# A two-layer attention, convolution and expert network on one core: the first attention scores are issued before the last two query tiles are rotated, and two normalisations are worked in halves of 256 tokens

## The reference

```python
def layer_norm(x, g, b):
    mu = xf.mean(-1, keepdims=True)
    var = jnp.square(xf - mu).mean(-1, keepdims=True)
    return (xf - mu) * lax.rsqrt(var + LN_EPS) * g + b
# each layer i
h = x * (1 + sc1) + sh1
mix = attention_mixer(...) if is_attn else short_conv_mixer(h, ...)
x = layer_norm(DEEPNORM_ALPHA * x + g1 * mix, ln_g[i, 0], ln_b[i, 0])
h = x * (1 + sc2) + sh2
ff = swiglu(h, w1, w3, w2) if is_dense else moe_swiglu(h, ...)
x = layer_norm(DEEPNORM_ALPHA * x + g2 * ff, ln_g[i, 1], ln_b[i, 1])
# in attention: q and k are rotated (apply_rope) before the scores q.k
```

## Time and profile before

| | |
|---|---|
| median of 3 runs | 2373.21 us (2371.28 to 2373.3) |
| time of the profiled execution | 2371.07 us |
| its span, first to last instruction | 2369.4 us |
| TensorE (PE) busy | 2256.5 us, 95% |
| PE weight loads | 1840.5 us, 78% |
| DVE / ACT / GpSimd busy | 62% / 46% / 14% |
| mean granted TensorE clock | 0.97 |

### The profile page before, as it was taken

One profiled execution on the slowest core, in us unless ns is written; L12 is line 12 of the kernel. 1 busy time (PEld: TensorE's weight loads), 2 busy tenths in 40 slices (PEclk: granted clock), 3 DMA queues, 4 the chain that ended last, 5 costly groups with the idle time before them and its releaser, 6 DMA issues.

```text
span 2369.4 us, 29554 instructions
## 1 busy us (share of the span) xinstructions
PE 2256.5 (95%) x11202; PEld 1840.5 (78%) x11203; DVE 1462.8 (62%) x1296; ACT 1096.2 (46%) x1084; POOL 324.9 (14%) x205
## 2 busy tenths in 40 slices
PE   6989999999998999798999999999999999999993
PEld 4866678888877888687888888888788788888782
DVE  3456655634566444897444454459999994544984
ACT  4135524222224222576343443347777774434763
POOL 0000026788852000100000000000000000000001
PEclk8999999999998999799999999999999999999997
DMA  7420083545442222798545554549999996454964
GB/s 306 190 107 1 1 339 125 195 167 187 178 146 92 100 89 89 288 379 308 213 177 195 187 209 179 198 183 398 360 394 366 394 371 230 179 193 177 359 261 143
DMA packets 76177, 512.71 MB, mean 216 GB/s; under 512 B 8241, under 2 KB 8369, under 8 KB 19025
## 3 DMA queue, kind: packets, MB, share of 16 engines
q1 hardware_dynamic: 61344, 442.46, 49.0%
q0 software_dynamic: 14768, 69.35, 8.0%
HBM read 482.41 MB, written 29.36 MB: 216 GB/s over the span
## 4 chain that ended last, share of the span: by engine, by line
PE 92%; DVE 4%; issue 1%; ACT 1%; DMA 1%; SPq 0%; DVEq 0%; ACTq 0%
PE ps L1672 27%; PE ps L1674 26%; PE ps L1673 26%; PE ps L562 2%; PE ps L517 2%; PE ps L573 2%; PE ps L2029 1%; DMA raw<-w_mod 1%; PE ps L1723 1%; PE ps L1774 1%; PE ps L521 1%; PE ps L1966 0%; DVE lo L1094 0%; PE ps L1822 0%; DVE zs L1267 0%
## 5 line engine op out<-in xcount | busy, mean ns | idle before, releaser
L1672 PE MATMUL ps<-ah,hi 128*128 128x512 f32 x688 | 270.4, 393 | 8.2 <-DVE al L1246 6.5
L1673 PE MATMUL ps<-al,hi 128*128 128x512 f32 x688 | 269.2, 391 | 0.0
L1674 PE MATMUL ps<-ah,lo 128*128 128x512 f32 x688 | 269.0, 391 | 0.0
L1538 DVE TENSOR_TENSOR he<-se,ps 128x512 f32<-128x512 f32 x112 | 77.0, 688 | 292.1 <-ACT se L993 291.8
L1295 DVE TENSOR_TENSOR lo<-raw,hi 128x2048 fp32r<-128x2048 f32 x112 | 255.9, 2284 | 0.0
L1672 PE MATMUL ps<-hia,xth 128*128 128x512 f32 x616 | 246.9, 401 | 6.9 <-issue 5.6
L1295 DVE TENSOR_TENSOR loa<-raw,hia 128x2048 fp32r<-128x2048 f32 x112 | 251.1, 2283 | 1.1 <-ACT hia L873 1.1
L1295 DVE TENSOR_TENSOR lob<-raw,hib 128x2048 fp32r<-128x2048 f32 x112 | 251.7, 2283 | 0.0
L993 ACT ACTIVATE se<-ps 128x512 f32<-128x512 f32 x112 | 67.0, 598 | 391.0 <-PE ps L1674 391.0
L1672 PE MATMUL ps<-hib,xth 128*128 128x512 f32 x616 | 245.4, 398 | 0.0
L1672 PE MATMUL ps<-hi,hh 128*128 128x512 f32 x616 | 240.5, 390 | 2.2 <-DVE hl L1542 1.5
(11 more groups left out here) (273 smaller groups left out, 3904.3 us busy)
## 6 DMA issues: line engine op xcount, KB each, us to landing
raw<-w_moe SPq DMA_DIRECT2D x336, 1024.0 KB, 5.4
raw<-w_pre SPq DMA_DIRECT2D x59, 1024.0 KB, 5.4
raw<-w_mod POOLq DMA_DIRECT2D x28, 1024.0 KB, 5.1
raw<-w_mod SPq DMA_DIRECT2D x20, 1024.0 KB, 7.5
dispatched_x<-zt POOLq DMA_DIRECT2D x22, 512.0 KB, 9.5
xg<-dispatched_x POOLq DMA_DIRECT2D x8, 1024.0 KB, 6.9
expert_y<-ys POOLq DMA_DIRECT2D x8, 1024.0 KB, 5.0
expert_y<-zt POOLq DMA_DIRECT2D x6, 512.0 KB, 24.6
```

What stands on the lines that cost most here:

```text
L1538: dve.tensor_tensor(HE[:], SE[:], up_view(q, 1), ALU.mult).then_inc(he_ready, 1)
L1672: pe.matmul(outp, wh, ah, start=first, stop=False, skip_group_check=True)
L1673: pe.matmul(outp, wh, al, start=False, stop=False, skip_group_check=True)
L1674: return pe.matmul(outp, wl, ah, start=False, stop=last, skip_group_check=True)
```

## The change

It touches the three places.

1. *Attention entry.* The last query unit writes banks 2 and 5 and TensorE goes on to the scores without waiting for its two rotations (`rope_done` 8 instead of 10; 10 is waited for at step 6, which first reads tile 6). The two `rope_tile` calls are issued by DVE in steps 1 and 2 of attention (`late`), the `split` of the first `o` unit in step 5. The last `mod_pair` and two `mod_cols` go behind the scores of step 1.
2. *Two normalisations by halves.* The last unit of `o` and of `dn2` is computed in four quarters (tokens 0 to 255 for both tiles, then tokens 256 to 511), of 24 matmuls of 256 tokens each. Residual, sums, squares, moments and the whole chain to `AL` run per half. `units_by_row_tile` runs once per half too, with matmuls of 256 tokens. `ZS` and `QS` now take in all 8 tiles, so 4 moment matmuls per half replace 24 in all.
3. *Moved splits.* The `split` of the next stage's second unit (slot 1) is issued before the tiles of the third unit of `o` and `dn2`; that of its first unit (slot 0) between the half tiles; ACT's `full_split` of the third unit between row tiles 5 and 6 of the second half. `scale_x` leaves the normalisation: in `up0` ACT does 8 half tiles after gated tile 1 and 8 after gated tile 2, in `conv` 16 before the third unit.

```diff
-        def attention_dve(dve, tn):
+        def attention_dve(dve, tn, late):
+                if s in late:
+                    late[s]()
-        def attention_pe(pe):
+        def attention_pe(pe, second_done):
-            pe.wait_ge(rope_done, 10)
+            pe.wait_ge(rope_done, 8)
+                if s == 6:
+                    pe.wait_ge(rope_done, 10)
+                if s == 1:
+                    second_done()
...
+                    late = {1: first_late, 2: lambda: rope_tile(2, Q[:, KD - 2, :], pair_free[1]),
+                            5: lambda: split(svs[0], svs[0])}
...
+            def last_unit(stage, gate):
+
+                half_tile(stage, 0, KD - 2, gate)
+                split(0, 0)
+                half_tile(stage, 0, KD - 1, gate)
+                half_tile(stage, 1, KD - 2, gate)
+                half_moments(stage, 0)
+                half_tile(stage, 1, KD - 1, gate)
+                dve.sem_inc(pair_free[1], 1)
+                half_norm(stage, 0)
+                half_norm(stage, 1)
...
+                        if name in ("o", "dn2") and j + 2 == ns:
+                            split(1, 1)
                         if lastpart and j + 1 == ns:
...
+            def half_stats(stage, h):
+                n = 2 * (stage - 1) + h + 1
+                if h == 0:
+                    pe.wait_ge(mod_free, t.n("mod"))
+                pe.wait_ge(stats_in, n)
+                for col, src in ((0, ZS), (1, QS)):
+                    for b in range(2):
+                        at = 4 * h + 2 * col + b
+                        ins = pe.matmul(PS[:, 7, at:at + 1], src[:, (2 * h + b) * BLK:(2 * h + b + 1) * BLK], mean_w[:, 0:1],
+                                        start=True, stop=True, skip_group_check=True)
                 ins.then_inc(stats_full, 1)
...
+            def unit_by_half(h, stage, ah, al):
+                for part in range(2):
+                    at = half_cols(part)
+                    for c in range(2):
+                        if part:
+                            pe.wait_ge(z_ready, n + KD - 2 + c + 1)
+                        for k in range(KD):
+                            ins = three(PS[:, 2 + c, at], hi[:, k, c * P:(c + 1) * P], lo[:, k, c * P:(c + 1) * P],
+                                        ah[:, k, at], al[:, k, at], k == 0, k == KD - 1)
+                        ins.then_inc(unit_done[h] if (part, c) == (1, 1) else part_done, 1)
+                        if (part, c) == (1, 0):
+                            half_stats(stage, 0)
+                half_rows(stage, 0)
...
+            def units_by_half(slots, part, stage):
+
+                half_stats(stage, 1)
+                units_by_row_tile(slots, part, (2 * stage - 1) * KD, half_cols(0), False, stage)
+                units_by_row_tile(slots, part, 2 * stage * KD, half_cols(1))
...
+                            if j in (1, 2):
+                                for k in range(KD):
+                                    scale_x(1, j - 1, k)
```

More of the change, by code:

```diff
@@ new lines, in normalised @@
+            def normalised(stage):
+                n = 2 * (stage - 1)
+                for k in (KD - 2, KD - 1):
+                    square(k, half_cols(0))
+                square(KD - 2, half_cols(1))
+                half_deviation(n + 1, 0)
+                square(KD - 1, half_cols(1))
+                for k in range(KD):
+                    if k == KD - 2:
+                        half_deviation(n + 2, 1)
+                    modulated(stage, 0, k)
+                for k in range(KD):
+                    modulated(stage, 1, k)
+                    if k == 5:
+                        full_split(2, 2)
@@ L918, in _ @@
                     full_split(0, 0)
+                    for h in range(2):
+                        for k in range(KD):
+                            scale_x(2, h, k)
                     done(2)
@@ L968, in _ @@
                         mod_part(1)
-                    if name in NORMS:
+                    if name in ("o", "dn2") and j + 1 == ns:
+                        normalised(NORMS[name])
+                    elif name in NORMS:
                         square(2 * j)
                         square(2 * j + 1)
[L972 to L978, removed]
+                if name == "co":
+                    deviation(5)
+            act.wait_ge(shift_ready, 5)
             for i in range(4):
@@ L1228, in norm @@
-                dve.wait_ge(rstd_rows, stage)
+                    dve.tensor_tensor(XZ[:, k, cols_], XZ[:, k, cols_], PS[:, bank, HALF:T], ALU.add).then_inc(xn_ready, 1)
+                dve.wait_ge(norm_rows, i + 1)
                 scaled(0)
-                dve.wait_ge(shift_rows, stage)
                 shifted(0)
@@ L1233, in norm @@
                 for k in range(1, KD):
+                    if h == 0 and k == KD - 2:
+                        half_moments(stage, 1)
                     if k + 1 < KD:
@@ L1313, in _ @@
                 elif name == "q":
-                    per = dict(ringp)
-                    per.update({"step": 6, "rope": 4, ("rel", id(pair_free[0])): 1, ("rel", id(pair_free[1])): 1})
-                    with t.loop(dve, count, per) as i:
+                    for i in range(count):
                         for j, h in enumerate(svs):
+                            if ns * i + j + 1 == ns * count:
+                                done(h)
+                                break
                             nx = svs[(j + 1) % ns]
@@ L1697, in unit_k, with units_by_row_tile @@
                 ins.then_inc(unit_done[h], 1)
-            def units_by_row_tile(slots, part, arrived):
+            def units_by_row_tile(slots, part, arrived, at=slice(0, T), last=True, rows=None):
                 for k in range(KD):
@@ new lines, in half_rows @@
+            def half_rows(stage, h):
+                pe.wait_ge(shift_ready, 2 * (stage - 1) + h + 1)
+                for part, src in enumerate((RSTD, SHIFTS)):
+                    for b in range(2):
+                        at = HALF * part + b * BLK
+                        ins = pe.matmul(PS[:, 6 - h, at:at + BLK], src[:, 2 * h + b:2 * h + b + 1].to_broadcast([P, P]), ident,
+                                        start=True, stop=True, skip_group_check=True)
+                ins.then_inc(norm_rows, 1)
@@ L1973, in _ @@
             spread(0, 0)
[L1974 removed]
+            pe.wait_ge(shift_ready, 5)
             spread(6, 1)
```

240 lines of the change are left out of this document (136 added, 104 removed).

## The result

| | before | changed |
|---|---|---|
| median | 2372.24 us (2369.53 to 2373.3, 4 runs) | 2356.11 us (2353.93 to 2356.76, 4 runs) |
| profiled execution: time, span | 2371.07, 2369.4 us | 2356.76, 2355.0 us |
| ratio | | 0.9943, 95% interval 0.9927 to 0.9959 |

The changed kernel is faster by 0.4 to 0.7%. The ratio is worth 13.5 us; the two medians alone differ by 16.1 us (0.9932), still inside the interval.

What follows compares the result with a forecast made beforehand. TensorE, busy 95% of the span, was taken as the bound, so only its idle or half-clock time could be won. Terms -6.5 + 0.4 + 0.6 - 0.5 = -6.0 us took the median from 2373.21 to 2367.2, range 2360.5 to 2372.

Steps and rivals of the forecast that it cites:

- Entry: Attention entry: scores follow the query products without idle time, some wait moving to step 3's row sums; -6.5 us.
- Normalisation 1: Last unit of o to third unit of up0: +51.2 us against 50.8 before, so +0.4 us.
- The late load: Normalisation 1: the weights for the moved split land 0.7 us after the unit's start.
- two gaps now draw the half clock [...]: +3: Normalisation 1: half clock after the gaps before the last quarter (0 to 2.2) and before up0 (1.5 to 2.4), +3 us.
- Normalisation 2: Last unit of dn2 to third unit of conv: 53.9 us against 54.4 before, so -0.5 us.
- The turns with GpSimd: Normalisation 2: DVE's moved split and sums alternate with GpSimd's operations, so TensorE stalls 7.5 us.
- +3 for the clock: Normalisation 2: 3 us for half clock, added to a chain ending at +50.9.
- `up0` behind it: Stage after normalisation 1: scale_x on ACT delays the fourth unit's split; +0.6 us with a margin for other waits.
- A: Both norms gain because tiles 4 and 5 are not delayed; sum about -16 us, 2357; chance 0.15.
- B: Both norms: clock gaps at the upper bound, plus 1 us for stalls between halves; sum -1.8, 2371.4; chance 0.20.
- C: Attention entry gives only -3, its stall moving to steps 3 to 6; sum -2.5 us, 2370.7; chance 0.08.
- D: Halved stages: 256-token streams never return to full clock; +46 us, 2413; chance 0.07.

Runs made afterwards that it cites:

- fill: The changed kernel with extra matmuls of 256 tokens in the two stalls before the third quarter (28 in o, 50 in dn2): 2357.74 us, ratio to before 0.9963.
- halves: The changed kernel with the attention entry (part 1) undone: 2361.57 us, ratio to before 0.9983.
- scale_back: The changed kernel with scale_x put back into the halved normalisation and out of up0 and conv: 2363.45 us, ratio to before 0.9979.
- late_split: The changed kernel with slot 1's split behind tile 7's first half, ACT's copy between the squares: 2349.41 us, ratio 0.9924; repeated as late_split_b: 2349.93 us, 0.9924.
- late_fill_b: Repeat run: late_split plus extra matmuls in three gaps (28 in dn2, 9 in o, 8 before each next stage): 2348.53 us, ratio to before 0.9919.

## Why the prediction was wrong

- *Entry, -6.5*: right in mechanism and size. The first pair of profiles gives 6.5, the means 7.0.
- *Normalisation 1, +0.4*: -1.6 in the first pair, -1.3 in the mean. The late load (+0.6), the split behind it and the stall (3.9 for 4.4) were as described; the first product of `up0` comes at +22.6 for +23.3, and without the clock the third unit stands at about +47.6 for +48.2 (`fill`, whose clock stayed up, has +47.5). **The failed term is "two gaps now draw the half clock [...]: +3".** It took 1.5 us here (343.87 to 370.44 are 26.6 us, in `halves`, whose clock stayed up there, 25.1) and none in `halves`: the first of the two falls was covered by DVE, and the second did not always come. Nor had the clock fallen "after every stop so far": in the kernel before TensorE stood still for 1.49 and 1.35 us ahead of 705.98 and 718.49, and the granted clock stayed at 1.00 until 733.43.
- *Normalisation 2, -0.5*: -5.0 in the first pair, -4.3 in the mean. The turns with GpSimd and the stall (6.8 for 7.5) were right. "+3 for the clock" was 0, 1.8 and 0.1 in the three profiles. **Here too the term "+3 for the clock" failed.** Another 1.3 is the sum of the chain: third unit at +49.6 without the clock, where +50.9 stood. Together the clock was charged 6 us in the two norms and took 1.6 on average.
- The working error behind it: I added the stretch of half clock to the end of the chain without asking, as I had for every other term, what runs beside it. The prediction's own times had DVE's `split` of slot 0 and the half tile beside the third quarter, 5.2 us of DVE against 2.9 (5.2 at half clock) of TensorE.
- *`up0` behind it, +0.6*: +1.2 in the mean; `scale_back`, without that work on ACT, has 340.1 against 341.4. Most of what the first profile has over that mean (342.0 for 341.4) is a turn that the prediction did not have there: DVE's `fl` took 4.09 us instead of 0.69 beside GpSimd, whose product ran from 551.19 to 554.80, and TensorE waited 1.21.

```profile
551.26 4.09 DVE L1439 TENSOR_TENSOR fl<-tmp,fh 128x512 f32 x1 [0.95 <-ACT fh L915]
...
555.40 0.50 PE L1768 MATMUL ps<-fh,hi 128*128 128x512 f32 x1 [1.21 <-DVE fl L1439]
```

  The Trainium skill (SBUF — State Buffer, "SBUF: two separate sides") says that the loser of the lock blocks for the whole instruction of the other; 4.09 for 0.69 us agrees.
- *Not in the sum*: the router, -2.9 in the first pair and -1.3 in the means. In the first pair its short matmuls ran at half clock for a shorter time (18.7 us against 22.3). Nothing there was changed, and one of the changed kernel's two profiles has 66.0; whether the halves bring this or chance does is open.
- *Rivals*: A had the size (2357) by a wrong way, since both stalls stand in the trace; its arrangement without the stall in norm 1 is nearly that of `late_split`, and gave 2349. B, the clock takes more, was the opposite of what happened. C and D did not occur: the entry gave its 6.5, and outside the falls named above the halves ran at 0.12 us and at full clock.
- *Range*: its low end counted half of A but no error in the clock term, which was bounded by 1.5 to 4.6 us a norm, and 0 was never among its values. With 0 for it the sum would have been -12.0, within 1.5 us of what both ratios say. That closeness is partly luck: the clock did take 1.6 us and `up0` 0.6 more than forecast, while the entry, the chains and the router, which was not in the sum, took less.

## What to carry to other kernels

Price a fall of TensorE's clock as one prices a wait: only what no other engine covers at that place counts, and filling a covered gap can move the fall to one that is not. Halving tiles halves the time an engine has between two rows, so the work that stood unseen between rows (here `scale_x` and a copy) decides whether halves pay at all: here neither was worth anything without the other. Where the list of one engine (here DVE, 14.6 of 16 us) leads to the next stage's first operand, do not put at its head an operation whose data come late: `late_split` leaves both splits in that list, ahead of the first `AL`, but the second now stands behind work whose operands are there, and that gave 5 us more than the change did.

## What was not expected of the hardware

- The clock fell at different places in executions of one program. The changed kernel's two profiles have 24.0 and 25.3 us from the first product of `conv` to the third unit, and the kernel before 27.0 and 25.4 us from the last unit of `o` to the first product of `up0`. Single runs of `late_fill_b` range from 2342.11 to 2353.54 us. Differences under 3 us need many runs or stretches of several profiles.
- The start of the program varies too: the last query product began between 130.2 and 134.1 us in fourteen profiles. One and the same kernel has 132.6 and 130.2 (`late_split`, `late_split_b`).
